# Upper slots of V filled earlier, whole-chunk remainders on VectorE, and one plain fp32 chunk in eight

## The chip, the cores and the metric

The kernel runs on one core of one Trainium2 chip. The metric is the device time of one execution in microseconds; of several runs the median is taken.

## The reference, cut to what matters

One inference step of a one-layer decoder: 264 live tokens (256 prompt tokens, 8 samples) and 16 meta tokens, everything in fp32. After attention, convolution and an output projection comes the PEER mixer, which is the part that the change touches:

```python
def peer_ffn(h, w_query, sub_keys, expert_u, expert_v):
    ...
        top_s, pos = lax.top_k(cand_s, PEER_TOPK)
        idx = jnp.take_along_axis(cand_i, pos, axis=-1)
        gate = jax.nn.softmax(top_s, axis=-1).astype(hc.dtype)
        act = jax.nn.gelu(jnp.einsum('cd,chkd->chk', hc, expert_u[idx]))
        return jnp.einsum('chk,chkd->cd', gate * act, expert_v[idx])
    ...
```

There are 16384 experts; each token takes 16 of them for each of 8 heads, so 128. `expert_u` and `expert_v` have one row of 2048 numbers for each expert.

## The kernel before, in words

**Stages.** The input projection, attention, the output projection and the query projection come first. Then stage U multiplies all of `expert_u` with the tokens, in 64 pairs of tiles (`PAIR_QRY` to `PAIR_U`), and stage V multiplies all of `expert_v` with weights W, from 1550.61 us to 2170.58 us. U and the projections cut their matrices into an fp32r rounded part (`hi`, made by ScalarE) and a remainder (`lo`, made by VectorE: raw minus `hi`), and run three products per tile.

**Stage V.** The tokens are in two kinds. For TD = 184 of them W is dense: 128 rows by 184 columns for each of 128 chunks of experts. For the other TG = 80 only the 128 chosen rows of `expert_v` are fetched by indirect DMA on GpSimd's queue (`gather_rows`, tile `gat`, a ring of ROWS = 4 buffers) and VectorE adds each into `gacc`, times the weight `gw` (`add_rows`, an "addition" below). These weights need words that GpSimd gathers too (`gather_u`, tile `gu`): 80 of them, one or two behind each of the first rows. GpSimd's order is fixed, and a row's gather waits until the addition four before it is done. V runs in two passes over the halves of the 2048 output columns, each with 128 chunks in 16 turns of 8 and 80 additions. All of `expert_v` passes through 8 slots of 512 KB: four in `raw`, which U uses too, and four upper ones in `raw_v`.

**A chunk on TensorE.** A split chunk is two quarters (`f`, L2225 and L2230): four matmuls of `hi` against the rounded and the remaining part of W side by side (368 columns), then four of `lo` against the rounded part of W (184 columns). A chunk whose number mod 8 is in `NATIVE` is plain (`plain`, L2240): eight products in plain fp32, each in two instructions, and neither ScalarE nor VectorE touches it. In both passes that is number 3 and number 7 of a turn; one of these is split all the same, the very last.

**What ScalarE and VectorE do beside it.** Their programs are written out in `halves`: at step k of a turn come the two quarters that lie 3 and 4 ahead (so the second quarter of the next chunk, and the first of the one after it), at each even k the parts of W for the chunk pair from k+2 on (`w_part`, tile `whl`), and then what `between` holds for this step: at k = 3 of pass 0's first four turns a product with counts (`times_up`), and at the steps listed in the table `ADDS` an addition. `hi` and `lo` have four buffers of a quarter each, so a quarter's parts may be written when TensorE is done with the quarter four before it. At the start of pass 1 the sums of pass 0 are added (L2119, turn 0), and in its turn 13 stand two reductions (L2129). Near the end of each pass TensorE multiplies `gacc` into the result (`row_sums`, L2212), between the products of the last quarters; it waits once for the last addition before that (`SUMS_AT`).

**What sets the order.** Each engine has one queue in program order. SP issues all loads; `load_expert` waits until a slot's former chunk is split (or, for a plain chunk, multiplied). `BOUNDS` and `WORDS_AT` say at the start of which turns the weights of which additions are made.

## Time and profile before

| | |
|---|---|
| median of 3 runs | 2191.46 us (2189.42 to 2191.72) |
| the profiled execution | 2187.61 us, its span 2185.9 us |
| TensorE busy | 2155.6 us, 99% |
| VectorE busy | 1618.8 us, 74% |
| ScalarE busy | 1120.7 us, 51% |
| GpSimd busy | 786.1 us, 36% |
| plain products of V (L2240) | 1008 instructions, 63 chunks |
| additions (L2094) | 160, 1278 ns each |
| remainders in V (L1627) | 383 records, 685 to 690 ns each |
| mean granted clock of TensorE | 0.991 of full |

The times of the profiled execution are read against its own 2187.61 us. Busy shares are means over stages with different limits: what stage V is worth is read from the timelines within it. A line such as L2225 is a line of the kernel before.

### The profile page before, as it was taken

To read this page: it belongs to the slowest core of one execution; us is meant where nothing else is said; L and a number is where in the kernel's file an instruction comes from. 1 tells how busy PE (TensorE), PEld (TensorE's weight loads), DVE (VectorE), ACT (ScalarE), POOL (GpSimd) and SP (SyncE) were. 2 spreads that over 40 slices of the span, in tenths; PEclk is the share of its full clock that TensorE was granted. 3 is DMA by queue.
4 is the path that set the end of the run, shared out by engine and by line. 5 is a ranking of instruction groups with operands and counts; after the bars stand their busy time and mean duration, and the time that the engine had idled before them with its cause. 6 is when DMAs were issued, how large, how long until landed. Compare 5 with 4: busy or idle time off the path is not lost.

```text
span 2185.9 us, 53083 instructions
## 1 busy us (share of the span) xinstructions
PE 2155.6 (99%) x16578; PEld 2123.5 (97%) x16578; DVE 1618.8 (74%) x2988; ACT 1120.7 (51%) x2094; POOL 786.1 (36%) x612
## 2 busy tenths in 40 slices
PE   9999999999999999999999999999999999999997
PEld 8999899999999999999999999999999999999997
DVE  8788788886766767888886444466588888888885
ACT  6445366667555444555555444444444444444453
POOL 0321100002011000588888888500377743222230
PEclk9999999999999999999999999999999999999997
DMA  7887756666555655777777877789899999999993
GB/s 247 290 290 250 238 179 196 190 214 216 186 187 191 192 167 180 190 190 181 190 191 188 191 187 186 186 272 287 275 378 378 372 390 400 327 370 369 367 370 142
DMA packets 302250, 546.01 MB, mean 250 GB/s; under 512 B 76896, under 2 KB 114232, under 8 KB 302016
## 3 DMA queue, kind: packets, MB, share of 16 engines
q1 hardware_dynamic: 225440, 427.67, 59.8%
q0 software_dynamic: 60064, 105.07, 16.1%
q10 hardware_dynamic: 16640, 12.06, 1.8%
q8 instruction: 41, 0.67, 0.1%
q14 instruction: 65, 0.53, 0.1%
HBM read 519.39 MB, written 25.28 MB: 249 GB/s over the span
## 4 chain that ended last, share of the span: by engine, by line
PE 66%; POOL 5%; issue 2%; DMA 2%; DVE 1%; ACT 0%; DVEq 0%; SPq 0%; ACTq 0%
PE ps L319 16%; PE ps L322 15%; PE ps L318 15%; PE ps L2225 8%; PE ps L2240 5%; PE ps L2230 5%; POOL gu L1801 3%; POOL gat L1643 2%; DMA gat<-expert_v,gidx 1%; DMA raw_v<-expert_v 0%; DMA raw<-weights 0%; PE ps L2212 0%; PE ps L1405 0%; DVE gacc L2094 0%; DVE lo L1627 0%
## 5 line engine op out<-in xcount | busy, mean ns | idle before, releaser
L306 DVE TENSOR_TENSOR lo<-raw,hi 128x512 fp32r<-128x512 f32 x995 | 685.6, 696 | 367.4 <-ACT hi L301 345.0
L301 ACT CAST hi<-raw 128x512 fp32r<-128x512 f32 x995 | 608.0, 619 | 472.7 <-PE ps L322 447.5
L318 PE MATMUL ps<-h_hi,hi 128*128 128x264 f32 (+1 forms) x3200 | 821.4, 286 | 1.6 <-DVE h_lo L959 1.6
L319 PE MATMUL ps<-h_lo,hi 128*128 128x264 f32 (+1 forms) x3200 | 820.2, 286 | 0.0
L318 PEld LDWEIGHTS ps<-h_hi,hi 128*128 128x128 f32 x3200 | 601.8, 188 | 9.0 <-issue 6.0
L319 PEld LDWEIGHTS ps<-h_lo,hi 128*128 128x128 f32 x3200 | 601.9, 188 | 0.0
L1784 POOL DMA_INDIRECT w_spill<-chosen,widx x256 | 432.4, 1689 | 264.8 <-DVE widx L2007 187.1
L322 PE MATMUL ps<-h_hi,lo 128*128 128x264 f32 (+1 forms) x3200 | 523.3, 285 | 2.0 <-DVE lo L306 1.8
L322 PEld LDWEIGHTS ps<-h_hi,lo 128*128 128x128 f32 x3200 | 444.3, 188 | 3.7 <-DVE lo L306 3.4
L2225 PE MATMUL ps<-whl,hi 128*128 128x368 f32 x1544 | 346.3, 345 | 4.6 <-DVE gacc L2094 2.8
L1643 POOL DMA_INDIRECT gat<-expert_v,gidx x160 | 179.6, 1123 | 285.2 <-DVE gacc L2094 269.6
L2225 PEld LDWEIGHTS ps<-whl,hi 128*128 128x128 f32 x1544 | 252.3, 192 | 6.0 <-DVE gacc L2094 3.1
L2230 PE MATMUL ps<-whl,lo 128*128 128x184 f32 x1544 | 227.9, 270 | 1.8 <-DVE lo L1627 1.6
L2230 PEld LDWEIGHTS ps<-whl,lo 128*128 128x128 f32 x1544 | 224.8, 191 | 3.3 <-DVE lo L1627 3.3
L2094 DVE SCALAR_TENSOR_TENSOR gacc<-gat,gw,gacc 128x1024 f32<-128x1024 f32 x160 | 204.5, 1278 | 9.0 <-DMA gat<-expert_v,gidx 9.0
L1622 ACT CAST hi<-raw_v 128x512 fp32r<-128x512 f32 x194 | 120.2, 620 | 163.7 <-PE ps L2230 120.4
L1622 ACT CAST hi<-raw 128x512 fp32r<-128x512 f32 x189 | 117.1, 620 | 160.3 <-PE ps L2230 109.7
L1627 DVE TENSOR_TENSOR lo<-raw,hi 128x512 fp32r<-128x512 f32 x189 | 127.1, 690 | 58.7 <-ACT hi L1622 50.7
L1627 DVE TENSOR_TENSOR lo<-raw_v,hi 128x512 fp32r<-128x512 f32 x194 | 128.0, 685 | 47.8 <-ACT hi L1622 47.7
L1801 POOL DMA_INDIRECT gu<-u_spill,gidx x80 | 91.1, 1139 | 177.1 <-issue 177.1
L1067 DVE SCALAR_TENSOR_TENSOR yc<-cv,dw,yc 128x256 f32<-128x256 f32 x240 | 107.1, 477 | 0.1
L1824 ACT ACTIVATE W<-ps 128x184 f32 (+1 forms) x128 | 41.4, 324 | 106.2 <-PE ps L322 105.8
(308 smaller groups left out, 2301.6 us busy)
## 6 DMA issues: line engine op xcount, KB each, us to landing
raw<-u_tiles SPq DMA_DIRECT2D x512, 256.0 KB
raw<-weights SPq DMA_DIRECT2D x480, 256.0 KB
raw_v<-expert_v SPq DMA_DIRECT2D x128, 512.0 KB
raw<-expert_v SPq DMA_DIRECT2D x124, 512.0 KB
w_spill<-zeros ACTq DMA_DIRECT2D x16, 736.0 KB, 5.7
wld<-w_spill SPq DMA_DIRECT2D x32, 368.0 KB, 4.1
u_spill<-ust SPq DMA_DIRECT2D x128, 40.0 KB
qb<-q_spill POOLq DMA_DIRECT2D x8, 512.0 KB, 6.0
```

Source lines behind the costliest of these rows:

```text
L301: nc.scalar.copy(hi[k % SPLIT][:], raw_quarter(k)).then_inc(hi_done, 1)
L306: nc.vector.tensor_tensor(lo[k % SPLIT][:], raw_quarter(k), hi[k % SPLIT][:].bitcast(F32), ALU.subtract).then_inc(lo_done, 1)
L318: pe.matmul(out, a, rhs[0][:, first + j, 0:n], start=start and j == 0, stop=False)
L319: pe.matmul(out, a, rhs[1][:, first + j, 0:n], start=False, stop=False)
L322: m = pe.matmul(out, lo[k % SPLIT][:, j], rhs[0][:, first + j, 0:n], start=False, stop=stop and j == QT - 1)
L1622: nc.scalar.copy(hi[q % SPLIT][:], expert_quarter(q)).then_inc(hi_done, credit(q))
L1627: nc.vector.tensor_tensor(lo[q % SPLIT][:], expert_quarter(q), hi[q % SPLIT][:].bitcast(F32), ALU.subtract).then_inc(lo_done, credit(q))
L1643: nc.gpsimd.indirect_dma_start(gat[n % ROWS][:], None, v_rows, bass.IndirectOffsetOnAxis(ap=index, axis=0)).then_inc(gat_in[n % ROWS], 16)
L1784: nc.gpsimd.indirect_dma_start(w_cells, bass.IndirectOffsetOnAxis(ap=widx[0:n, t, hd, k:k + 1], axis=0), chosen[0:n, 2, t, hd, k:k + 1], N ...
L2094: nc.vector.scalar_tensor_tensor(out=gacc[:, g], in0=gat[b][:], scalar=gw[:, j:j + 1], in1=gacc[:, g], op0=ALU.mult, op1=ALU.add).then_inc ...
L2225: pe.matmul(ps[:, bank(QT * r + j), 0:2 * TD], a[:, j], whl[k // 2 % 2][:, k % 2].rearrange("p a n -> p (a n)"), start=start, stop=False, ...
L2230: m = pe.matmul(ps[:, bank(QT * r + j), 0:TD], b[:, j], whl[k // 2 % 2][:, k % 2, 0], start=False, stop=stop, skip_group_check=True)
```

## The change

Three things are changed. The first loads of the upper slots (chunks 4 to 7 of V) are issued in the last four pairs of U instead of at V's start; they count on semaphores of their own (`piece_in`, which the input's pieces used before). In V the remainder of a chunk is one subtraction over both its quarters, at the place where its second quarter's stood; only the first quarters of V stay as they were. And `NATIVE` is `(7,)`: chunk 3 of every turn is split. Beside these the additions are spread in another way (`ADDS`), and so are the turns in which their weights are made.

```diff
-NATIVE = (3, 7)
+NATIVE = (7,)
...
-    BOUNDS = (1, 2, 4, 7, 10, 13)
+    BOUNDS = (1, 2, 4, 6, 8, 11)
     FIVE, SIX = (1, 2, 3, 5, 6), (1, 2, 3, 5, 6, 7)
-    ADDS = [[(), (3, 5, 6, 7)] + 6 * [FIVE] + 6 * [SIX] + [FIVE, (0, 1, 2, 3, 4)], 15 * [FIVE] + [(0, 1, 2, 3, 4)]]
-    WORDS_AT = (0, 5, 15, 30, 50, 65, TG)
+    AT_END = (0, 1, 2, 3, 4)
+    ADDS = [[(), (2, 3, 5, 6, 7)] + [SIX if i in (4, 7, 9, 11, 13) else FIVE for i in range(2, 15)] + [AT_END],
+            [SIX if i in (3, 8, 12) else FIVE for i in range(15)] + [AT_END[0:2]]]
+    WORDS_AT = (0, 5, 15, 30, 40, 55, TG)
...
     def expert_lo(dve, q):
+        if q % 2 == 0:
+            return
         dve.wait_ge(hi_done, 2 * C0 + q + 2 * RAW + 1)
         dve.wait_ge(mm_done, 2 * C0 + q + 1)
-        nc.vector.tensor_tensor(lo[q % SPLIT][:], expert_quarter(q), hi[q % SPLIT][:].bitcast(F32),
-                                ALU.subtract).then_inc(lo_done, credit(q))
+        if q < AHEAD + 1:
+            nc.vector.tensor_tensor(lo[q % SPLIT][:], expert_quarter(q), hi[q % SPLIT][:].bitcast(F32),
+                                    ALU.subtract).then_inc(lo_done, credit(q))
+            return
+        both = slice((q - 1) % SPLIT, q % SPLIT + 1)
+        rows = expert_slot(q // 2 % SLOTS).rearrange("p (r j) n -> p r j n", r=2)
+        nc.vector.tensor_tensor(lo_parts[:, both], rows, hi_parts[:, both].bitcast(F32),
+                                ALU.subtract).then_inc(lo_done, 1 + credit(q))
...
+        def upper_in(s):
+            sp.dma_start(expert_slot(s).rearrange("p a b -> p (a b)"), expert_v[0, s]).then_inc(expert_in(s), 16)
+
+        def weighed_pair(i, upper=None):
             for s in range(RAW):
                 load_half(sp, 4 * i + s, s, u_tiles[4 * (i - PAIR_QRY) + s])
...
+                if s == 0 and upper:
+                    upper_in(upper)
+        with sp.Fori(PAIR_W, PAIR_U - 4) as i:
+            weighed_pair(i)
+        for i in range(PAIR_U - 4, PAIR_U - 1):
+            weighed_pair(i, RAW + i - PAIR_U + 4)
```

On SP's queue at the end of U and the start of V stood, before, these rows (`raw<-expert_v` of 128x512 are half-chunk loads of chunks 0 to 3, `raw_v<-expert_v` loads of the upper slots, `ust` and `wld` U's results and counts):

```order
L1669 DMA u_spill<-ust_76 128x80
L291 DMA raw<-expert_v 128x512 x4
L1669 DMA u_spill<-ust_77 128x80
L291 DMA raw<-expert_v 128x512 x4
L1669 DMA u_spill<-ust_76 128x80
L1672 DMA wld<-w_spill 128x4x184
L1739 DMA raw_v<-expert_v 128x1024
L1669 DMA u_spill<-ust_77 128x80
L1739 DMA raw_v<-expert_v 128x1024 x2
L1739 DMA raw<-expert_v 128x1024 x3
L1739 DMA raw_v<-expert_v 128x1024
L1672 DMA wld<-w_spill 128x4x184
```

Now the last pair of U has this, with the last of the four upper loads behind the first half-loads of the pair:

```order
L1687 DMA wld<-w_spill 128x4x184
L292 DMA raw<-u_tiles 128x512 x2
L1719 DMA raw_v<-expert_v 128x1024
L292 DMA raw<-u_tiles 128x512 x2
L1684 DMA u_spill<-ust_71 128x80
L1687 DMA wld<-w_spill 128x4x184
L292 DMA raw<-u_tiles 128x512 x4
L1684 DMA u_spill<-ust_70 128x80
L292 DMA raw<-expert_v 128x512 x4
L1684 DMA u_spill<-ust_71 128x80
L292 DMA raw<-expert_v 128x512 x4
L1684 DMA u_spill<-ust_70 128x80
```

and right behind it follow:

```order
L1687 DMA wld<-w_spill 128x4x184
L1764 DMA raw<-expert_v 128x1024
L1684 DMA u_spill<-ust_71 128x80
L1764 DMA raw<-expert_v 128x1024 x2
L1687 DMA wld<-w_spill 128x4x184
L1764 DMA raw<-expert_v 128x1024
```

So no load of chunks 4 to 7 stands behind U's last results any more, and SP goes on with chunks 8 to 15.

On VectorE, the first part of a turn of pass 1 with five additions (all such turns read alike; `whl` of 128x2x184 are the parts of W for two chunks, of 128x184 for one):

```order
L1627 TENSOR_TENSOR lo_57<-raw,hi_53 128x512
L1627 TENSOR_TENSOR lo_54<-raw,hi_50 128x512
L2086 TENSOR_TENSOR whl_160<-W,whl_160 128x184
L1627 TENSOR_TENSOR lo_55<-raw,hi_51 128x512
L2094 SCALAR_TENSOR_TENSOR gacc<-gat_151,gw,gacc 128x1024
L1627 TENSOR_TENSOR lo_54<-raw_v,hi_50 128x512
L2086 TENSOR_TENSOR whl_159<-W,whl_159 128x2x184
L2094 SCALAR_TENSOR_TENSOR gacc<-gat_164,gw,gacc 128x1024
L1627 TENSOR_TENSOR lo_55<-raw_v,hi_51 128x512
L1627 TENSOR_TENSOR lo_56<-raw_v,hi_52 128x512
L2094 SCALAR_TENSOR_TENSOR gacc<-gat_165,gw,gacc 128x1024
L1627 TENSOR_TENSOR lo_57<-raw_v,hi_53 128x512
```

and the same part now, from the end of the turn before it:

```order
L1642 TENSOR_TENSOR lo<-raw,hi 128x1024 x2
L2108 TENSOR_TENSOR whl_154<-W,whl_154 128x2x184
L1642 TENSOR_TENSOR lo<-raw,hi 128x1024
L2116 SCALAR_TENSOR_TENSOR gacc<-gat_147,gw,gacc 128x1024
L1642 TENSOR_TENSOR lo<-raw,hi 128x1024
L2108 TENSOR_TENSOR whl_153<-W,whl_153 128x2x184
L2116 SCALAR_TENSOR_TENSOR gacc<-gat_145,gw,gacc 128x1024
L1642 TENSOR_TENSOR lo<-raw_v,hi 128x1024
L2116 SCALAR_TENSOR_TENSOR gacc<-gat_158,gw,gacc 128x1024
L1642 TENSOR_TENSOR lo<-raw_v,hi 128x1024
L2108 TENSOR_TENSOR whl_154<-W,whl_154 128x184
```

Between two additions there stands now one subtraction over 1024 elements where two over 512 stood, and chunk 3, which was passed over, has its subtraction and its part of W too.

## Rows read from the trace of the kernel before

**Rows 1.** Busy time by stage: span, each engine's busy us, clock, DMA share, GB/s.

```profile
1444.10:1455.80 11.70, 11.70 (x99) 11.70 (x98) 9.39 (x14) 6.51 (x14) 0.00 (x0) 1.00 1.04 355
1502.60:1514.30 11.70, 11.70 (x98) 11.70 (x97) 7.98 (x11) 5.76 (x13) 0.00 (x0) 1.00 0.91 281
1900.00:1950.00 50.00, 50.00 (x350) 50.00 (x349) 40.99 (x57) 22.73 (x43) 14.18 (x14) 1.00 1.02 366
```

**Rows 2.** Timeline of TensorE in pass 1: start, length, line, operation, count.

```profile
1904.70 2.68 PE L2240 MATMUL ps<-W,raw 128*128 x16
...
1907.09 0.97 PE L2225 MATMUL ps<-whl,hi 128*128 128x368 f32 x4
...
1909.45 0.86 PE L2225 MATMUL ps<-whl,hi 128*128 128x368 f32 x4
1910.15 0.59 PE L2230 MATMUL ps<-whl,lo 128*128 128x184 f32 x4
...
1913.93 2.68 PE L2240 MATMUL ps<-W,raw_v 128*128 x16
```

**Rows 3.** Timeline of TensorE in V's first turn.

```profile
1570.61 4.12 PE L2240 MATMUL ps<-W,raw_v 128*128 128x184 f32 x16 [3.82 <-DMA raw_v<-expert_v]
```

**Rows 4.** Timeline of GpSimd while it gathers rows and words.

```profile
1576.15 0.99 POOL L1801 DMA_INDIRECT gu<-u_spill,gidx  x1 [0.30 <-issue]
...
1586.71 1.15 POOL L1643 DMA_INDIRECT gat<-expert_v,gidx  x1 [9.57 <-DVE gacc L2094]
...
1745.57 0.94 POOL L1643 DMA_INDIRECT gat<-expert_v,gidx  x1 [0.30 <-issue]
```

**Rows 5.** Timeline of VectorE: row additions 0, 45 and 47 of pass 0.

```profile
1585.17 1.28 DVE L2094 SCALAR_TENSOR_TENSOR gacc<-gat,gw,gacc 128x1024 f32<-128x1024 f32 x1
...
1745.65 1.28 DVE L2094 SCALAR_TENSOR_TENSOR gacc<-gat,gw,gacc 128x1024 f32<-128x1024 f32 x1 [1.26 <-DMA gat<-expert_v,gidx]
...
1752.43 1.28 DVE L2094 SCALAR_TENSOR_TENSOR gacc<-gat,gw,gacc 128x1024 f32<-128x1024 f32 x1 [0.39 <-DMA gat<-expert_v,gidx]
```

**Rows 6.** Timeline of TensorE: first and last chunk of turn 10.

```profile
1743.42 0.97 PE L2225 MATMUL ps<-whl,hi 128*128 128x368 f32 x4
...
1761.46 0.81 PE L2240 MATMUL ps<-W,raw_v 128*128 x4
```

**Rows 7.** Timeline of VectorE in pass 1, a turn with five additions.

```profile
1904.48 0.69 DVE L1627 TENSOR_TENSOR lo<-raw_v,hi 128x512 fp32r<-128x512 f32 x1 [1.38 <-ACT hi L1622]
...
1905.09 0.53 DVE L2086 TENSOR_TENSOR whl<-W,whl 128x368 fp32r<-128x368 f32 x1
...
1905.54 1.28 DVE L2094 SCALAR_TENSOR_TENSOR gacc<-gat,gw,gacc 128x1024 f32<-128x1024 f32 x1
...
1906.74 1.28 DVE L1627 TENSOR_TENSOR lo<-raw_v,hi 128x512 fp32r<-128x512 f32 x2
...
1910.34 0.34 DVE L2086 TENSOR_TENSOR whl<-W,whl 128x184 fp32r<-128x184 f32 x1
```

**Rows 8.** Timeline of ScalarE in the same turn.

```profile
1904.35 0.50 ACT L1834 CAST whl<-W 128x368 fp32r<-128x368 f32 x1
...
1909.72 0.62 ACT L1622 CAST hi<-raw_v 128x512 fp32r<-128x512 f32 x1 [0.28 <-PE ps L2230]
```

**Rows 9.** Timeline of VectorE in turn 13 of pass 1.

```profile
2113.91 2.21 DVE L2129 TENSOR_REDUCE total<-half_sum 128x132 f32<-128x1056 f32 x1
```

**Rows 10.** Timeline of TensorE: row sums of pass 0, then of pass 1.

```profile
1851.89 0.60 PE L2225 MATMUL ps<-whl,hi 128*128 128x368 f32 x2 [0.24 <-DVE gacc L2094]
...
1853.97 0.53 PE L2225 MATMUL ps<-whl,hi 128*128 128x368 f32 x2
...
2152.37 0.98 PE L2225 MATMUL ps<-whl,hi 128*128 128x368 f32 x2 [2.52 <-DVE gacc L2094]
...
2156.27 0.87 PE L2225 MATMUL ps<-whl,hi 128*128 128x368 f32 x2
```

**Rows 11.** Busy time by stage, row sums of pass 1.

```profile
2156.20:2160.00 3.80, 3.80 (x18) 3.80 (x18) 0.69 (x1) 0.62 (x1) 0.00 (x0) 0.50 0.02 4
```

More of the change, by code:

```diff
@@ L1731, in load_expert @@
             m = NK * p + 8 * i + s
-            first = isinstance(i, int) and p == 0 and i == 0
-            back = m - (RAW if first else SLOTS)
+            back = m - SLOTS
             if native(back if isinstance(i, int) else s + SLOTS):
```

35 lines of the change are left out of this document (18 added, 17 removed).

## Prediction

> **What bounds the kernel now.** I read the busy time by stage first. In U's last pairs and in V TensorE is busy all the time at full clock [rows 1]; so it sets the end, except where it stands still. VectorE is busy 41 of 50 us in V, the nearest of the others. Then I read TensorE's timeline in V for what one chunk costs and for each place where it stops, and then, at these places, the engine that it waits for.
>
> A half turn is 9.23 us: three split chunks of 2.24 us (two from 1909.45 to 1913.93), and the rest, 2.51 us, is the plain chunk, which ends at 1907.09 and makes the group behind it 0.11 longer [rows 2]. A turn is 18.46 us.
>
> TensorE stops for long at three places. In V's first turn chunk 7 is not there: 3.82 us of idle time, and its products then take 4.12 us instead of 2.68 [rows 2, 3]: 5.3 us. Around turn 10 it waits for VectorE, and VectorE for gathered rows [rows 5]. Before the last row sums it waits 2.52 us for the last addition, and the quarters behind that take 3.90 us where the same in pass 0 take 2.08 [rows 10], at a granted clock of 0.50, so 1.2 GHz [rows 11].
>
> **What the change does, part by part.**
>
> *Early upper slots.* They take the first stop away. What they add to U is one load of 512 KB in each of four pairs of 11.70 us, 45 GB/s on top of 281, where the same mix ran at 355 GB/s without TensorE waiting [rows 1]. I take 0 for U. That V's first turn is 5.3 us shorter is true, but a later part gives it no use:
>
> *The pace of the gathers.* GpSimd issues a row every (1745.57 - 1586.71) / 43 = 3.69 us, since one or two words stand between rows, and in this whole stretch it waits for nobody (0.30 us between its instructions) [rows 4]. It starts at 1586.71 because it waited 9.57 us for addition 0, which ran at 1585.17 [rows 4, 5]. Now addition 0 stands one step earlier in a turn that begins 5.3 us earlier with one more cheap chunk, so at about 1576; then GpSimd's own last word (1576.15 + 0.99 + 0.30) sets the start, 1577.4, 9.3 us earlier. But the new table wants more from it: in turns 1 to 9 stand 48 additions instead of 46. At 3.69 us each, the last of turn 9 is now number 47, issued at 1577.4 + 158.9 = 1736.3. Before, number 47 ran 6.86 us after its issue, having waited for the landing [rows 4, 5]: that gives 1743.2, and I take 1 us more, since its landing was a quick one. Turn 10 can begin 0.5 us ahead of that addition: behind it stand 1.20 (its time to the next instruction, 1906.74 - 1905.54 [rows 7]), the subtraction for the turn's second chunk, 1.27, and 0.1 for loading, against 2.35 + 0.70 us after which TensorE wants it [rows 2]. So turn 10 begins at about 1743.7; before it began at 1743.42 [rows 6]. **Up to turn 10: +0.3 us** (bounds -1 and +2). The 5.3 us, and all that turns 1 to 9 might gain, are gone, spread over many short waits for rows.
>
> Turn 10 took 1761.46 + 2.39 - 1743.42 = 20.43 us [rows 2, 6], 2 us of it stalls, since VectorE was behind. The gathers of words are over by now in the new order, so it is a usual turn: **-1.9 us**.
>
> *A usual turn after the change.* For TensorE it is 7 x 2.24 + 2.51 = 18.19, 0.27 less. Whether it gets that depends on VectorE. A subtraction over 512 holds VectorE 0.61, an addition 1.20, parts of W 0.45 for two chunks, 0.26 for one [rows 7]. A subtraction over 1024 isn't in the trace. Above it is bounded by two of 512, 1.22. The step between 128x184 and 128x368 is 0.19 for 184 elements, so 0.53 for 512; twice that with no fixed part at all is 1.06, the bound below. I take 0.61 + 0.53 = 1.14, and its result is there 0.08 later, as with the others. The Trainium skill, VectorE: DVE Perf Modes, section on the TRN2 errata, gives (N + 151) / 0.96 ns for the whole length of such an fp32 operation, 1.22 us; by it nothing in the sum would be different.
>
> So VectorE does 7 x 1.14 + 3 x 0.45 + 0.26 + 5 x 1.20 = 15.6 us in 18.2: it fits. But in steps 1 to 3 it has 3 x (1.14 + 1.20) + 0.45 = 7.5 us to do in 6.7, and its head start is small, as the remainder of a chunk's first quarter now comes only with the second: that can't begin before TensorE has left the chunk two back, plus 0.27 and 0.62 for ScalarE's `hi` [rows 8]. With the turn's start as 0, TensorE begins its chunks at 0, 2.35, 4.59, 6.83, 9.07 and so on. Step 1: subtraction 3.30 to 4.44, addition to 5.64. Step 2: to 6.78; then it waits for ScalarE's part of W, which follows a `hi` that waits for the first quarter of chunk 2 (5.71 + 0.27 + 0.52 + 0.50 = 7.00) [rows 8]; to 7.50, addition to 8.70. Step 3: subtraction from 8.70, to be read at 9.97. TensorE wants it at 9.07 + 0.70 = 9.77, better 0.1 before. **It stalls for about 0.35 us once in a turn**; in step 4 there is no addition and VectorE catches up. The turn is 18.54, against 18.46: +0.08. A sixth addition at step 7 falls into slack. Bounds: 18.19 (no stall) and 18.8 (two more near misses of 0.1).
>
> Turns 11 to 15 of pass 0 and 16 of pass 1 remain. 17 of them are usual: **+1.4 us**. The rest by the same walk: pass 0's last turn, with additions at steps 0 to 4, stalls 1.0: +0.5. Pass 1's first, with four sums of 0.6 us between: stalls 1.3: +1.1. Its turn 13, with two reductions of 2.1 us [rows 9], in which VectorE starts late by 0.9, 0.1, 0.6, 0.1 and 1.3 us: 2.9 of stalls, +2.3. The last, almost without additions: -0.3. **Together +3.6 us.**
>
> *The end.* Only two additions stand in the last turn, at steps 0 and 1, so the wait of 2.52 us before the row sums is gone. Without that gap the clock shouldn't fall: in pass 0 the same products, entered after 0.24 us of idle time, run in 2.08 us a quarter [rows 10]. Four quarters give 4 x 1.82 = 7.3: **-9.8 us**.
>
> **The sum:** +0.3 - 1.9 + 1.4 + 3.6 - 9.8 = -6.4 us, from 2187.61 to 2181.2 for an execution like the profiled one. That one stands 3.85 us below the median; from the median it is 2185.0.
>
> **The rivals.**
>
> *VectorE keeps up* (20%): the walk is too strict by some tenths, which is all that it needs. Then 18 turns gain 0.35 each and the special ones half of theirs: -8, so 2177. For it: VectorE is idle 18% of the time. Against it: the same walk through the old turn puts its second addition 7.7 us behind the turn's start (1904.70 - 6.84), and there the trace has it, at 1905.54 [rows 2, 7].
>
> *The gathers don't hold V back* (10%): landings come sooner or GpSimd issues faster. Then most of the 5.3 us and of nine turns' 0.2 are kept: 2179. Against it: GpSimd had no gap to give [rows 4].
>
> *The clock falls at the end all the same* (10%): +7.3, so 2192. The Trainium skill, TensorE: Matmul & The Clock Gate, Part 1, says that the clock falls behind idle time and comes back with sustained work; by this it would stay up here, and the trace agrees: 0.50 behind the gap of 2.52 us [rows 11].
>
> *The late remainder costs more* (15%), the one on the slower side: as TensorE waits for both quarters' remainder before the first quarter's second group, any delay of `hi`, of a row's landing or of an addition is handed on undamped, where the old order had over 1 us to spare. If a usual turn is 19.1 instead of 18.54 and the special ones double: +10 + 3, so 2198. From 19.0 on it decides: the change is then slower.
>
> **How the numbers follow.** My own case has 45% and its range is 2180 to 2190. No change that a measurement of this kernel can tell is within 0.2%, 2187.1 to 2195.8. Below that lie six tenths of my case and the first two rivals, 0.57, less a little for both: 0.55. Above lie the last rival and a part of the clock's: 0.17. The range 2174 to 2197 leaves out the ends of the first and the last rival.
>
> **What would show it.** In the profile after: no wait of TensorE for `raw_v`; GpSimd's fifth row at about 1577 and its 48th at about 1736, and TensorE waiting for `lo` in turns 2 to 9, with turn 10 beginning near 1743.7; from there turns of 18.5 us with one wait for `lo` each, in the fifth chunk; a pass 1 turn 13 of 21 us; no wait before the last row sums, and quarters of 2.1 us there. It would be wrong if the turns were 18.2 or 19 us, if turn 10 began before 1740, or if the clock at the end were 0.50.

## The result, and the profile after the change

The changed kernel took 2200.1 us (median; 2194.8 to 2210.7, apart from one run of 9209), the kernel before, beside it, 2189.9 us. The ratio is 1.0052, with a 95% interval of 1.0042 to 1.0062: **slower**, by 0.5%, 10.2 us between the two medians. The forecast was 2185.0 us, with a range up to 2197: wrong in its sign, and outside its range. The profiled execution took 2199.36 us with a span of 2197.6; before it was 2187.61 and 2185.9, so the two traces differ by 11.8 us, 1.6 more than the medians, and can be laid side by side.

I read in the order in which the forecast went. First TensorE's timeline in V's first turns (start, length, line, operation, count, and in brackets the idle time ahead and who ended it), the rows that answer to [rows 3]:

```profile
1581.35 0.69 PE L2252 MATMUL ps<-whl,lo 128*128 128x184 f32 x4 [0.67 <-DVE lo L1642]
1596.96 1.16 PE L2252 MATMUL ps<-whl,lo 128*128 128x184 f32 x4 [6.07 <-DVE lo L1642]
```

No wait for `raw_v` is left: the first turn's chunk 7 is there when it is wanted. But in turn 2 stands a stop of 6.07 us, longer than the one removed. It is for a remainder, and VectorE, which makes it, shows why it is late:

```profile
1587.12 1.22 DVE L1642 TENSOR_TENSOR lo<-raw,hi 128x1024 fp32r<-128x1024 f32 x1
1593.76 1.28 DVE L2116 SCALAR_TENSOR_TENSOR gacc<-gat,gw,gacc 128x1024 f32<-128x1024 f32 x1 [5.42 <-DMA gat<-expert_v,gidx]
1595.68 1.23 DVE L1642 TENSOR_TENSOR lo<-raw,hi 128x1024 fp32r<-128x1024 f32 x1
```

The fifth addition waited 5.42 us for its row (row 4, counted from 0), and the subtraction queued behind it came with it. Behind this stop the granted clock is down as well, 0.57 on the mean from 1597 to 1603 us (length, each engine's busy us, clock, DMA share, GB/s):

```profile
1597.00:1603.00 6.00, 6.00 (x26) 6.00 (x27) 3.91 (x4) 1.88 (x4) 4.78 (x5) 0.57 0.93 256
```

A group of products with the rounded part takes 1.49 us there, elsewhere 0.86. So the next view is GpSimd's timeline, the rows that answer to [rows 4]:

```profile
1576.08 1.72 POOL L1823 DMA_INDIRECT gu<-u_spill,gidx  x1 [0.30 <-issue]
1578.11 1.66 POOL L1658 DMA_INDIRECT gat<-expert_v,gidx  x1 [0.31 <-issue]
1580.08 3.43 POOL L1823 DMA_INDIRECT gu<-u_spill,gidx  x1 [0.30 <-issue]
1583.81 0.94 POOL L1823 DMA_INDIRECT gu<-u_spill,gidx  x1 [0.30 <-issue]
1585.06 0.95 POOL L1658 DMA_INDIRECT gat<-expert_v,gidx  x1 [0.30 <-issue]
...
1748.85 1.96 POOL L1658 DMA_INDIRECT gat<-expert_v,gidx  x1 [0.30 <-DVE gacc L2116]
```

GpSimd waits for nobody (0.30 us between instructions), yet row 4 is issued at 1585.06, where 1577.4 was forecast, and row 47 at 1748.85 instead of 1736.3. Its instructions have become long: 1.72, 1.66, one of 3.43. The groups of instructions say it for the whole kernel, before (first fence) and after: 1123 and 1534 ns for the same gather (count, then busy us and mean ns of one). Most of this rise stands where the rows aren't awaited: over rows 4 to 47 alone the mean is 1.19 us before and 1.26 after, over pass 1 it is 1.11 and 1.67.

```profile
L1643 POOL DMA_INDIRECT gat<-expert_v,gidx x160 | 179.6, 1123 | 285.2 <-DVE gacc L2094 269.6 <-issue 15.5
```

```profile
L1658 POOL DMA_INDIRECT gat<-expert_v,gidx x160 | 245.5, 1534 | 224.4 <-DVE gacc L2116 208.8 <-issue 15.5
L1642 DVE TENSOR_TENSOR lo<-raw,hi 128x1024 fp32r<-128x1024 f32 x126 | 153.8, 1222 | 15.8 <-ACT hi L1629 14.8 <-PE ps L2252 0.6
L1642 DVE TENSOR_TENSOR lo<-raw_v,hi 128x1024 fp32r<-128x1024 f32 x97 | 118.5, 1221 | 6.3 <-ACT hi L1629 4.6
```

Second, TensorE around turn 10 and in a usual turn of pass 1, the rows that answer to [rows 6] and [rows 2]. The 16 products of a plain chunk end a turn:

```profile
1753.94 2.68 PE L2262 MATMUL ps<-W,raw_v 128*128 x16
1756.33 0.97 PE L2247 MATMUL ps<-whl,hi 128*128 128x368 f32 x4
...
1909.59 2.68 PE L2262 MATMUL ps<-W,raw_v 128*128 x16
1911.98 0.97 PE L2247 MATMUL ps<-whl,hi 128*128 128x368 f32 x4
...
1921.11 0.86 PE L2247 MATMUL ps<-whl,hi 128*128 128x368 f32 x4
1922.04 0.69 PE L2252 MATMUL ps<-whl,lo 128*128 128x184 f32 x4
...
1928.26 2.06 PE L2262 MATMUL ps<-W,raw_v 128*128 x12
```

Turn 10 begins at 1756.33, against 1743.42 before [rows 6]. The usual turn is 1928.26 - 1909.59 = 18.67 us, against 18.46. Its products need 18.19; the rest are small waits, of which the largest is at 1922.04, in the fifth chunk: products of the remainder that begin 0.93 us behind the group ahead of them, where the others begin 0.70 behind. With the slower group behind it, this one costs 0.33 us.

Third, the end, the rows that answer to [rows 10]:

```profile
2172.40 0.56 PE L2234 MATMUL ps<-same,gacc 128*128 128x16 f32 x4
...
2174.41 0.56 PE L2234 MATMUL ps<-same,gacc 128*128 128x16 f32 x4
...
2176.42 0.55 PE L2234 MATMUL ps<-same,gacc 128*128 128x16 f32 x4
```

A quarter takes 2.01 us where it took 3.90, nothing waits ahead of them, and the granted clock between 2172 and 2182 is 1.00.

So the change's own gain at the end is there, and what is lost lies in turns 1 to 9, and in small pieces behind.

### The profile page after: what moved, and what is told of

Same layout as the page of the kernel before. It is cut to its first block and busy times, and to the rows that moved or that the text cites. A ratio compares the mean times of both kernels' runs of the same rounds, so it can differ in the third digit from the quotient of the medians.

```text
span 2197.6 us, 52837 instructions
## 1 busy us (share of the span) xinstructions
PE 2154.8 (98%) x16578; PEld 2102.6 (96%) x16578; DVE 1650.6 (75%) x2829; ACT 1165.3 (53%) x2158; POOL 859.3 (39%) x612
## 5 line engine op out<-in xcount | busy, mean ns | idle before, releaser
L307 DVE TENSOR_TENSOR lo<-raw,hi 128x512 fp32r<-128x512 f32 x995 | 686.0, 697 | 366.2 <-ACT hi L302 342.9
L302 ACT CAST hi<-raw 128x512 fp32r<-128x512 f32 x995 | 608.0, 619 | 471.8 <-PE ps L323 445.2
L2247 PE MATMUL ps<-whl,hi 128*128 128x368 f32 x1800 | 393.8, 340 | 0.8 <-DVE whl L2108 0.5
L1658 POOL DMA_INDIRECT gat<-expert_v,gidx x160 | 245.5, 1534 | 224.4 <-DVE gacc L2116 208.8
L2252 PEld LDWEIGHTS ps<-whl,lo 128*128 128x128 f32 x1800 | 255.3, 191 | 45.5 <-DVE lo L1642 38.9
L2252 PE MATMUL ps<-whl,lo 128*128 128x184 f32 x1800 | 274.3, 274 | 22.5 <-DVE lo L1642 20.4
L2247 PEld LDWEIGHTS ps<-whl,hi 128*128 128x128 f32 x1800 | 289.8, 191 | 1.1 <-DVE whl L2108 0.7
L1629 ACT CAST hi<-raw 128x512 fp32r<-128x512 f32 x253 | 156.8, 620 | 205.5 <-PE ps L2252 160.9
L1642 DVE TENSOR_TENSOR lo<-raw,hi 128x1024 fp32r<-128x1024 f32 x126 | 153.8, 1222 | 15.8 <-ACT hi L1629 14.8
L1642 DVE TENSOR_TENSOR lo<-raw_v,hi 128x1024 fp32r<-128x1024 f32 x97 | 118.5, 1221 | 6.3 <-ACT hi L1629 4.6
L2108 DVE TENSOR_TENSOR whl<-W,whl 128x368 fp32r<-128x368 f32 (+1 forms) x128 | 63.1, 493 | 60.5 <-PE ps L2252 49.1
```

Source lines behind the costliest of these rows:

```text
L302: nc.scalar.copy(hi[k % SPLIT][:], raw_quarter(k)).then_inc(hi_done, 1)
L307: nc.vector.tensor_tensor(lo[k % SPLIT][:], raw_quarter(k), hi[k % SPLIT][:].bitcast(F32), ALU.subtract).then_inc(lo_done, 1)
L1629: nc.scalar.copy(hi[q % SPLIT][:], expert_quarter(q)).then_inc(hi_done, credit(q))
L1642: nc.vector.tensor_tensor(lo_parts[:, both], rows, hi_parts[:, both].bitcast(F32), ALU.subtract).then_inc(lo_done, 1 + credit(q))
L1658: nc.gpsimd.indirect_dma_start(gat[n % ROWS][:], None, v_rows, bass.IndirectOffsetOnAxis(ap=index, axis=0)).then_inc(gat_in[n % ROWS], 16)
L2247: pe.matmul(ps[:, bank(QT * r + j), 0:2 * TD], a[:, j], whl[k // 2 % 2][:, k % 2].rearrange("p a n -> p (a n)"), start=start, stop=False, ...
```

## The experiments

Two suspects, both of one edit, the single subtraction for a whole chunk. **Theory 1**: VectorE's longer instruction holds off GpSimd, so that rows come late while they set the pace. **Theory 3**: TensorE gets the first quarter's remainder half a microsecond later, and stalls in each turn. Against both, **theory 2**: GpSimd is late because the change asks more of it and of VectorE. The runs went in four sets, each beside runs of the kernel before on its own chip. The chips differ: the kernel before took 2188.8 us in the first set, 2197.4, 2197.8 and 2195.9 in the others (the last two sets are one chip). So ratios are compared, and places in the traces. A ratio is of medians; a place in a trace (the last four columns) is of one execution.

| run | set | ratio to before (95%) | row 4 issued | turn 9's plain chunk | usual turn, pass 1 | gather, mean ns |
|---|---|---|---|---|---|---|
| before | | 1 | 1586.71 | 1741.03 | 18.45 | 1123 |
| the change | | 1.0052 (1.0042-1.0062) | 1585.06 | 1753.94 | 18.67 | 1534 |
| two subtractions | 1 | 0.9963 (0.9949-0.9978) | 1577.29 | 1742.76 | 18.19 | 1406 |
| single subtraction alone | 1 | 1.0061 (1.0042-1.0080) | 1584.64 | 1745.74 | 18.67 | 1362 |
| back to back | 1 | 0.9973 (0.9959-0.9987) | 1578.28 | 1747.53 | 18.19 | 1302 |
| early slots + additions | 1 | 0.9958 (0.9945-0.9971) | 1578.48 | 1744.89 | 18.45 | 1170 |
| late release | 2 | 0.9993 (0.9981-1.0006) | 1576.78 | 1746.24 | 18.88 | 1209 |
| single from turn 10 | 2 | 0.9986 (0.9972-0.9999) | 1577.90 | 1743.21 | 18.67 | 1446 |
| later demand | 2 | 0.9963 (0.9947-0.9980) | 1578.26 | 1737.77 | 18.19 | 1339 |
| the change again | 3 | 1.0019 (1.0003-1.0035) | 1583.21 | 1752.48 | 18.67 | 1492 |
| rounded parts first | 3 | 1.0015 (0.9997-1.0033) | 1577.26 | 1750.95 | 18.66 | 1623 |
| plain 3, later demand | 3 | 0.9956 (0.9939-0.9973) | 1576.66 | 1737.22 | 18.45 | 1132 |
| additions alone | 3 | 0.9978 (0.9963-0.9994) | 1583.56 | 1752.59 | 18.45 | 1131 |
| single up to turn 9 | 4 | 1.0018 (1.0001-1.0035) | 1583.66 | 1754.69 | 18.19 | 1339 |
| early slots alone | 4 | 0.9979 (0.9963-0.9995) | 1578.89 | 1737.89 | 18.45 | 1123 |
| two subtractions again | 4 | 0.9964 (0.9947-0.9980) | 1577.78 | 1746.33 | 18.19 | 1355 |
| early slots + additions again | 4 | 0.9948 (0.9929-0.9967) | 1574.63 | 1741.71 | 18.45 | 1162 |

**Two subtractions.** The change without the single subtraction:

```diff
-        if q % 2 == 0:
-            return
...
-        nc.vector.tensor_tensor(lo_parts[:, both], rows, hi_parts[:, both].bitcast(F32),
-                                ALU.subtract).then_inc(lo_done, 1 + credit(q))
+        nc.vector.tensor_tensor(lo[q % SPLIT][:], expert_quarter(q), hi[q % SPLIT][:].bitcast(F32),
+                                ALU.subtract).then_inc(lo_done, credit(q))
```

> The change whole, but the rounded parts are again subtracted a quarter at a time (128x512), as before the change. Theory 1 (the one 128x1024 subtraction of 1.22 us holds off GpSimd's gather instructions, so that rows are issued and land later in the turns in which the rows set the pace): a gather's instruction falls back from 1534 ns to about 1.14 us in pass 0 and 1.1 us in pass 1, row 47 of pass 0 is issued by about 1737 instead of 1748.85, turn 10 begins by about 1744 instead of 1756.3, the usual turn of pass 1 is 18.1 to 18.4 us instead of 18.67, and the end keeps its clock: 2177 to 2181 us. Theory 2 (GpSimd is slow because the change asks it for rows sooner, and VectorE has one more split chunk a turn to serve): the gather's instruction stays above 1.3 us and turn 10 begins at 1752 or later: 2190 to 2198 us.

2177.95 us, 0.9963: the single subtraction turns a gain of 0.37% into a loss of 0.52%. Row 4 is issued at 1577.29, as forecast for the change:

```profile
1577.29 1.15 POOL L1649 DMA_INDIRECT gat<-expert_v,gidx  x1 [0.58 <-DVE gacc L2107]
1578.74 1.14 POOL L1814 DMA_INDIRECT gu<-u_spill,gidx  x1 [0.30 <-issue]
1580.18 2.96 POOL L1814 DMA_INDIRECT gu<-u_spill,gidx  x1 [0.30 <-issue]
```

But theory 1 had more to say and missed: the gather's mean is 1406 ns, not 1.1 us, and row 47 comes at 1741.04, not 1737. The gather's mean over the kernel is no measure of the loss: here it is 1.58 us in pass 1, where GpSimd waits for VectorE anyhow, and 1.10 us over rows 4 to 47. Nor is the one of 3.43 us the change's own: one of 2.96 stands here too, but behind row 4. The 11.2 us by which turn 9's plain chunk comes sooner than in the change (1742.76 against 1753.94) are 7.8 at row 4, nothing in the 43 rows behind it (163.75 and 163.79 us), and 3.4 between row 47 and that chunk.

**The single subtraction alone**, on the kernel before (the same lines the other way round, and the buffers of `hi` and `lo` side by side).

> The kernel before, with the one 128x1024 subtraction for a chunk as the only change: chunks 3 and 7 stay plain, the table of additions and the late upper slots stay as they were. Theory 1: a gather's instruction rises from 1123 ns to 1.35 us or more, more so in pass 1, and turn 10 begins 6 us or more later than 1743.42: 2194 to 2202 us in all. Theory 2: the gather's instruction stays within 0.05 us of 1123 ns, VectorE has 0.12 us a chunk less to do, and the time is that of before within 3 us.

2198.81 us, 1.0061. Theory 1's time, with turn 9's plain chunk 4.7 us later than before (6 or more were expected) and the usual turn 18.67 instead of 18.45, although two plain chunks a turn leave VectorE more time. Theory 2, by which this kernel would be as fast as before, has fallen.

**Early slots and additions**, with chunk 3 left in plain fp32 (`NATIVE = (3, 7)`) and two subtractions.

> The kernel before with the early upper slots and the new table of additions; the subtraction stays a quarter at a time and chunk 3 stays in plain fp32. Theory 1: gathers at about 1.14 us, no stop for raw_v in the first turn, turn 10 begins by 1744, the end keeps its clock (about 9.8 us gained there): 2178 to 2183 us. Theory 2: the new table asks for rows sooner than GpSimd has them, gathers above 1.3 us, turn 10 at 1750 or later: 2186 to 2194 us.

2178.68 us, 0.9958: gathers short (1170 ns), no stop for `raw_v`, the end at full clock. Turn 9's plain chunk is at 1744.89, later than I expected, since rows are still short in number: VectorE waited 4.26 us for row 23. But whether TensorE's turn is 18.45 or 18.19 us, the two kernels without the single subtraction are within 0.1% of each other in this set.

**Two subtractions, back to back.** The waits of the change, its instruction cut in two:

```diff
+        for r in range(2):
+            one = slice((q - 1) % SPLIT + r, (q - 1) % SPLIT + r + 1)
+            nc.vector.tensor_tensor(lo_parts[:, one], rows[:, r:r + 1], hi_parts[:, one].bitcast(F32),
+                                    ALU.subtract).then_inc(lo_done, credit(q) if r else 1)
```

> The change whole, but the subtraction of a chunk is given as two instructions of 128x512, one straight after the other once the whole chunk is rounded: the waits and their order are those of the change, only the length of one instruction is halved (0.67 us each). If the length of the single instruction holds GpSimd off (theory 1 in its narrow form), a gather's instruction falls to 1.2 us or less and the time to 2178 to 2186 us. If what holds it off is the unbroken stretch in which VectorE subtracts, however many instructions it is made of (theory 1 in its wide form), the gather's instruction stays at 1.4 us or more and the time at 2197 to 2203. If the loss is that the first quarter's remainder comes late to TensorE (theory 3), it is 2198 to 2204 too, with gathers that have become short.

2181.57 us, 0.9973: nearly all is back, though VectorE does more (its gathers, at 1302 ns, are longer than the 1.2 us that I had named). It isn't the wait for the whole chunk's rounding that costs, but that one instruction does both quarters.

**Late release.** The same two instructions, but neither quarter is released until both are done (`then_inc(lo_done, 1 + credit(q))` on the second alone).

> As the run with two subtractions back to back (2181.6 us), but the first quarter's remainder is released only with the second's, as in the change; each instruction stays 128x512. In the last runs a usual turn of pass 1 was 18.19 us with that quarter released after the first of the two, and 18.67 in the change. Theory 3 (the late remainder holds TensorE): the usual turn is 18.7 to 18.8 us, 0.08 us of VectorE more than the change per chunk, and the whole 2195 to 2202 us. Theory 1 (only GpSimd's delay by the long instruction counts): the usual turn stays at 18.19 and the whole near 2182.

The usual turn goes from 18.19 to 18.88 us: theory 3, by itself. The rows are on time (row 4 at 1576.78, gathers of 1209 ns). The time, 0.9993, lies between. In VectorE's timeline of this run the subtraction that TensorE waits for stands behind a part of W and an addition, with no idle time between them:

```profile
1970.69 0.54 DVE L2112 TENSOR_TENSOR whl<-W,whl 128x368 fp32r<-128x368 f32 x1 [0.47 <-issue]
1971.15 1.28 DVE L2120 SCALAR_TENSOR_TENSOR gacc<-gat,gw,gacc 128x1024 f32<-128x1024 f32 x1
1972.35 1.29 DVE L1644 TENSOR_TENSOR lo<-raw_v,hi 128x512 fp32r<-128x512 f32 x2
```

```profile
1972.34 0.86 PE L2251 MATMUL ps<-whl,hi 128*128 128x368 f32 x4
1973.69 0.69 PE L2256 MATMUL ps<-whl,lo 128*128 128x184 f32 x4 [0.49 <-DVE lo L1644]
```

The first of the two takes 0.69 us from 1972.35 and would have served TensorE at 1973.04; it was told at the end of both. In the change, with one instruction of 1.22 us instead of 1.29, it is the same with a little less.

**The single subtraction only from turn 10 on**, and its complement, **only up to turn 9** (`q >= 16 * 10`, and `q < 16 * 10`, as the condition for it).

> The change, with the single subtraction of a chunk only from pass 0's turn 10 on; up to there a quarter at a time. If the loss has two parts, turns 1 to 9 (rows late) and 0.48 us in each turn after, then turns 1 to 9 go as in the run with two subtractions (turn 10 begins by about 1746 instead of 1756.3), the usual turn of pass 1 is 18.67, its turns 13 and 14 take 42.7 together, and the whole is 2186 to 2190 us. If the single subtraction costs only where rows set the pace: 2177 to 2181. If it costs only behind turn 10: 2197 to 2200.

> The change with the single subtraction of a chunk only in turns 0 to 9 of pass 0, a quarter at a time from turn 10 on: the complement of the run with it from turn 10 on only. If the two costs add up: turn 10 begins at 1752 to 1757 as in the change (1756.3 and 1754.9 in its two profiles) against 1745 to 1747 without it, row 4 is issued at 1583 to 1585, the usual turn of pass 1 is 18.19 us, its turn 13 20.7; the span is 8 to 10 us above that of the run with two subtractions, 12 to 13 below the change's. If the rows' lateness has nothing to do with the single subtraction, turn 10 begins by 1747 and the span is that of two subtractions.

The traces part cleanly. Up to turn 9's plain chunk the first stands where two subtractions stand (1743.21 and 1742.76), the second where the change does (1754.69 and 1753.94, against 1746.33 for two subtractions in its own set: 8.4 us). From there to the plain chunk of turn 14 of pass 1 the first takes 2148.90 - 1743.21 = 405.7 us, two subtractions 2136.49 - 1742.76 = 393.7; the second takes 396.6, and two subtractions in its set 398.1. The change's trace against that of two subtractions in the first set is 11.2 us later up to there and loses 10.2 more behind: in the traces there are two costs, of like size. The medians don't part them as cleanly. They give 0.54% (1.0018 against 0.9964) up to turn 9, and about 0.22% (0.9986 against 0.9964, from two chips) behind. But on the last chip the change itself has 1.0019, no more than the run up to turn 9: there the medians show nothing of the second cost. And the traces of these two runs are of quick executions: up to turn 9, 2192.88 us, the fastest of its twelve and 5.7 below their median; from turn 10 on, 2190.42 us, 4.2 below. Of the totals, the first was forecast 5 us too low (2186 to 2190, measured 2194.6); the second's span, 2191.1, is 7.2 us above two subtractions, near the 8 to 10 expected, but only 4.8 below the change again, not 12 to 13: on that chip two subtractions lose something behind turn 10 that the change doesn't, of which more below.

**Gathers beside VectorE**, the disputed cost by itself.

> A kernel of its own, which computes nothing of the reference (its outputs are zeros): seven stretches, in each of which GpSimd issues eight indirect gathers of 128 rows of 1024 while VectorE (1) rests, (2) subtracts 128x512 from SBUF 24 times without a pause, (3) subtracts 128x1024 12 times without a pause, (4) 128x512 with a pause after each, (5) 128x1024 with a pause after each, (6) subtracts 128x512 with one input from PSUM, without a pause, (7) makes the addition's operation 128x1024 without a pause. Theory 1: 0.94 us a gather at rest; beside a VectorE that never pauses each gather is held to the end of the run or for several us (2, 3, 7 alike); with pauses 1.1 to 1.3 us beside 128x512 and 1.4 to 1.7 beside 128x1024; and 0.94 in (6) if it is the second SBUF input that holds it. Theory 2 (GpSimd isn't touched by VectorE): 0.94 in all.

GpSimd's timeline, with one gather of each of the stretches 1 (at rest), 3 (128x1024, no pause), 4 (128x512, pauses) and 5 (128x1024, pauses):

```profile
10.82 0.94 POOL L56 DMA_INDIRECT gat<-v,idx  x1 [0.31 <-issue]
...
56.62 1.96 POOL L62 DMA_INDIRECT gat<-v,idx  x1 [0.30 <-issue]
...
78.78 1.32 POOL L65 DMA_INDIRECT gat<-v,idx  x1 [0.30 <-issue]
...
94.14 1.18 POOL L68 DMA_INDIRECT gat<-v,idx  x1 [0.30 <-issue]
```

At rest a gather takes 0.94 us; beside subtractions of 128x1024 without a pause 1.97, and 1.97 + 0.30 is two of VectorE's steps (12 of them span 13.7 us, 1.14 each): every gather ends 0.94 us into a subtraction, as if it had stood still until that one began. Theory 1 has its mechanism. But two of my numbers missed. A VectorE that never pauses doesn't lock GpSimd out, and beside 128x512 without a pause, or the additions without a pause, one gather in eight was held (1.38 us) and the others took 0.94: two steps of 128x512 (24 took 14.8 us, 0.62 each) or one addition (12 took 14.7, 1.23) are nearly GpSimd's own step at rest, 1.24, so that it falls in step. What a hold costs hangs on how two rhythms meet. That also left one thing unproved: all gathers beside the input from PSUM took 0.93 or 0.94, but at the same rhythm as those that were hardly held anyway. So a second kernel put both inputs side by side.

> As the run of gathers beside VectorE, computing nothing of the reference (outputs are zeros). Eight gathers in each of seven stretches, beside a VectorE that (1) rests, (2) subtracts 128x1024 without a pause, second input from PSUM, (3) the same, both inputs from SBUF, (4) and (5) the same two with a pause after each, (6) and (7) 128x512 from PSUM and from SBUF with a pause after each. If the second SBUF input holds GpSimd off: 0.94 us a gather in 1, 2, 4 and 6; 1.97 in 3; about 1.18 in 5; 0.94 and 1.32 in turn in 7. If the rhythm or the output's writing does it, whatever the input: 2 as 3, 4 as 5, 6 as 7.

The groups of its gathers, in the order of the stretches 2 to 7 (each is line, count, busy us, mean ns of one):

```profile
L59 POOL DMA_INDIRECT gat<-v,idx x8 | 7.5, 937 | 20.9 <-DMA gat<-v,idx 18.8 <-issue 2.1
L62 POOL DMA_INDIRECT gat<-v,idx x8 | 13.0, 1626 | 9.5 <-DMA gat<-v,idx 7.4 <-issue 2.1
L65 POOL DMA_INDIRECT gat<-v,idx x8 | 7.5, 936 | 8.1 <-DMA gat<-v,idx 5.9 <-issue 2.1
L68 POOL DMA_INDIRECT gat<-v,idx x8 | 9.6, 1200 | 10.1 <-DMA gat<-v,idx 8.0 <-issue 2.1
L71 POOL DMA_INDIRECT gat<-v,idx x8 | 7.5, 936 | 8.4 <-DMA gat<-v,idx 6.3 <-issue 2.1
L74 POOL DMA_INDIRECT gat<-v,idx x8 | 9.2, 1144 | 9.8 <-DMA gat<-v,idx 7.6 <-issue 2.1
```

Input from PSUM 937, 936, 936 ns; from SBUF, at the same width and rhythm, 1626, 1200 and 1144. It is the second input in SBUF that holds GpSimd off, in these runs until the instruction underway is over. In the kernel a gather can be held longer: the one of 3.43 us began at 1580.08, beside a subtraction, outlasted that one, a part of W and a second subtraction, and ended 0.91 us into the addition behind them. Why it wasn't let in sooner isn't shown. The Trainium skill (SBUF — State Buffer, section "Who interferes with whom") says that a VectorE instruction with two SBUF inputs contends with a GpSimd instruction that reads SBUF, and these runs agree. The same section infers that such a subtraction doesn't stall a DMA that GpSimd issues; here the measurement decides otherwise.

**Rounded parts first.** The change, with TensorE's order in a split chunk turned round, so that it wants the first remainder later:

```diff
+        def both_first(c, k):
+            pe.wait_ge(wlo_done, c + 1)
+            for r in range(2):
+                pe.wait_ge(hi_done, 2 * C0 + 2 * c + r + 2 * RAW + 1)
...
+            pe.wait_ge(lo_done, 2 * C0 + 2 * c + 1 + 2 * RAW + 1)
+            for r in range(2):
```

> The change, with TensorE's order inside a split chunk turned round in turns 1 to 14 of both passes: first the products of the rounded part for both quarters, then those of the remainder for both; so TensorE wants the first remainder 0.75 us later. VectorE's single subtraction is as in the change. Theory 3 (0.48 us a turn comes from TensorE having to wait for a remainder that the single subtraction brings late): the usual turn of pass 1 falls from 18.67 to 18.19 us, and what stays of the loss is turns 1 to 9 with rows that come late (gathers still long, 1.5 to 1.7 us in pass 1): 0.999 to 1.002 of before. If the 0.48 us come from something else in VectorE (its total load), the turn stays at 18.67 and the ratio at 1.005.

A miss: the usual turn stayed at 18.66, the ratio at 1.0015 (the change in its set: 1.0019). VectorE's timeline tells what happened. In this run's usual turn, which begins at 1913.44, its second part of W is at

```profile
1916.78 0.54 DVE L2108 TENSOR_TENSOR whl<-W,whl 128x368 fp32r<-128x368 f32 x1 [0.80 <-ACT whl L1856]
```

which is 3.34 us after the turn's start; in the change it was

```profile
1914.65 0.54 DVE L2108 TENSOR_TENSOR whl<-W,whl 128x368 fp32r<-128x368 f32 x1 [0.35 <-PE ps L2252]
```

2.67 us after it. TensorE wants the remainder 0.75 later, but it also lets go of the first quarter's buffers that much later, so ScalarE's `hi`, its part of W, and VectorE behind them all begin later. What the one end gained the other lost. That TensorE's wait for a remainder told late is what lengthens the turn is so shown only by the late release, beside the run back to back: the same instructions, and 18.88 us against 18.19.

**Later demand**: two subtractions, five additions in each of turns 1 to 9 and six in each of turns 10 to 14 (`8 * [FIVE] + 5 * [SIX]`), and the same with chunk 3 in plain fp32.

> The change without the single subtraction, and with the sixth additions moved behind turn 9: five additions in each of turns 1 to 9 (45 instead of 48) and six in each of turns 10 to 14 of pass 0. In the run with two subtractions turns 0 to 9 took 16 us more than ten of 18.19, with rows at 3.8 us each. If the rows' demand sets these stops, three rows fewer are worth 3 x 3.8 = 11 us less what the six additions a turn cost VectorE behind: turn 10 begins about 1737 to 1740, and the whole is 2168 to 2174 us. If the stops come from VectorE's own load or from single late rows, turn 10 begins as before (1745) and the whole is 2176 to 2180.

> The early upper slots and the new table of additions without the single subtraction and with chunk 3 in plain fp32, and the table as in the run with later demand: five additions in each of turns 1 to 9, six in each of turns 10 to 14. There turn 10 began 5 us earlier, but each of turns 10 to 14 took 19.3 us instead of 18.19, since VectorE had six additions beside fourteen subtractions. With twelve subtractions a turn it should keep up: turn 10 begins at about 1740, turns 10 to 14 take 18.46 to 18.7, and the whole is 0.993 to 0.995 of before (with the table of the change: 0.9958). If VectorE still falls behind: 0.996.

The rows' part came out: turn 9's plain chunk at 1737.77 and 1737.22, 5.0 and 7.7 us sooner than with the change's table (1742.76, 1744.89). Both gave it back: turns 10 to 14 took 18.5 to 20.3 us in the first, turns 11 to 14 19.5 to 20.5 in the second. In the second the last turn of pass 0 and the first of pass 1 took 24.9 us each as well, where the kernel before has 20.7 and 21.0. I had put that down to VectorE and its six additions, and expected the second to be free of it (0.993 to 0.995) and the first to take 2168 to 2174 us, 0.991 to 0.993 of before. The waits from 1757 to 1856 us, of the first and of the second, say otherwise:

```profile
ACT hi L1628 <- DMA raw<-expert_v: 28.6, 17, 3.7
ACT hi L1628 <- DMA raw_v<-expert_v: 15.0, 15, 1.4
```

```profile
ACT hi L1628 <- DMA raw_v<-expert_v: 25.5, 14, 3.8
ACT hi L1628 <- DMA raw<-expert_v: 21.6, 12, 3.7
```

ScalarE waits for the expert chunks themselves. A turn loads eight of 512 KB, and with six rows of the same size it asks more of the DMA engines than with five. Measured are 0.9963 and 0.9956, and neither beats the change's own table.

**The change again, the additions alone, the early slots alone**, and the two best once more.

> The change itself once more, on the chip of the runs beside it, since the chips differ: before had a median of 2188.8 us in one set of runs and 2197.4 in another. Expected 1.003 to 1.007 of before, and the same places of loss: row 4 issued about 8 us later than in the run with two subtractions back to back and late release (1576.8), usual turns of pass 1 at 18.67 us.

> The kernel before with the new table of additions alone (the upper slots filled late, as before; two subtractions a chunk; chunk 3 plain). The end should keep its clock and lose its wait (9.8 us gained), the stop for raw_v in the first turn stays, row 4 is issued no earlier than 1577, and the two additions more in turns 1 to 9 cost up to 7 us of stops: 0.997 to 1.000 of before, against 0.9958 with the early upper slots as well. If the early slots are given no use, it is 0.996.

> The kernel before with the early upper slots alone: the table of additions is that of before, chunk 3 plain, two subtractions. The prediction says that the 3.8 us stop for raw_v goes, but that the rows, which GpSimd issues at its own pace from addition 0 on, give it back by turn 10. Addition 0 then still stands at step 3 of turn 1, so row 4 is issued at about 1581 to 1582 (1586.71 less the 5.3 us), and turn 10 begins 5 us earlier, at 1738 to 1739, if GpSimd is carried forward with it: 0.9975 of before. If it is given back: turn 10 at 1743 and 0.999 to 1.001. The end stays at 1.2 GHz with its wait of 2.5 us.

> The change with two subtractions a chunk, once more on this chip: 0.9963 of before if the gain is the kernel's and not the chip's. If expert loads land late on this chip (ScalarE waiting for raw and raw_v, as in the last runs with later demand), a turn of 18.19 us asks for more than one of 18.67 and part of the gain is lost: 0.997 to 0.999.

> The early upper slots and the new table of additions alone, once more on this chip: 0.9958 of before, equal to the run with two subtractions within 0.1%, since there the 0.27 us a turn of chunk 3 went into waits for rows and for VectorE. Its turns are 18.46 us.

The change keeps its absolute time, 2200.3 us, while the kernel before is 9 us slower here than in the first set; hence 1.0019, below what I expected. What differs, two subtractions on this chip show: they keep turns of 18.19 us up to turn 7 of pass 1, and then take 18.2 to 20.4 where the first set had 18.19. The waits between 2010 and 2120 us, of this run and then of the change again:

```profile
ACT hi L1628 <- DMA raw<-expert_v: 27.4, 19, 4.2
ACT hi L1628 <- DMA raw_v<-expert_v: 14.2, 14, 1.6
```

```profile
ACT hi L1629 <- PE ps L2252: 40.4, 52, 2.8
DVE whl L2108 <- PE ps L2252: 10.1, 10, 1.4
```

The first waits for expert loads, the second for TensorE. Busy time from 2010 to 2120 us, of two subtractions in the first set and here (length, each engine's busy us, clock, DMA share, GB/s):

```profile
2010.00:2120.00 110.00, 108.75 (x760) 107.48 (x759) 102.84 (x142) 64.58 (x123) 46.85 (x32) 1.00 1.01 384
```

```profile
2010.00:2120.00 110.00, 106.75 (x728) 103.64 (x727) 96.91 (x133) 58.68 (x114) 35.93 (x30) 1.00 1.01 372
```

The DMA engines are busy all the time in both, and bring 384 GB/s on one chip and 372 on the other, where the loads come late. The share alone doesn't tell this: it is 1.00 as well in the change again, which moves 363 GB/s on that chip and doesn't wait for loads. So a turn of 18.19 us asks for more than one of 18.67, and I take it that this chip hadn't more to give; that the chip is the cause, and not the execution, is argued and not shown. Whether the kernel before loses its 9 us there in the same way wasn't traced. The ratio didn't suffer: 0.9964, where I had expected 0.997 to 0.999 if the loads came late.

The additions alone (0.9978) and the early slots alone (0.9979) multiply to 0.9957; together they measured 0.9958 and 0.9948 (the second 0.16% below two subtractions in its set, where 0.1% at most was expected). In the additions alone turn 9's plain chunk begins at 1752.59, 11.6 us later than before and nearly as late as in the change, though their gathers are short (1131 ns): their row 4, behind the stop for `raw_v`, is issued at 1583.56, and the new table wants two rows more. So a late row 4 is enough for this loss, whatever makes it late, and beside the new table the early slots do have a use: they bring row 4 to 1578.48 and 1574.63, and the chunk to 1744.89 and 1741.71. With the early slots alone row 4 was issued at 1578.89, sooner than I had it (1581 to 1582), and turn 9's plain chunk is 3.1 us sooner than before, where 5 were expected if GpSimd is carried along and none if not: the truth is between. The best of all kernels is thus **the early slots and the new table, without the single subtraction and with chunk 3 left in plain fp32**: 2178.68 us in the first set, 0.42% (0.52% in the last) below the kernel before. Splitting chunk 3 as well makes TensorE's turn 0.26 us shorter and brings nothing (0.9963, 0.9964).

## Why the prediction was wrong, point by point

In pieces of the profiled execution, the change against before, with the forecast in brackets: up to turn 10 +12.9 us (+0.3); turn 10 itself -1.3 (-1.9); sixteen usual turns +3.8 (+0.08 each, +1.4 for seventeen); pass 0's last +0.4 (+0.5), pass 1's first +0.8 (+1.1); its turn 13 +3.1 (+2.3), turn 14 +2.4 (a usual one); the rest to the end -10.4 (-9.8 and -0.3). The sum is +11.7, against 11.75 measured (2199.36 - 2187.61).

- **The step that failed is the pace of the gathers**, +0.3 us, in which GpSimd's instructions keep their length whatever VectorE does. Of its error of 12.6 us, 7.7 are the restart: row 4 at 1585.06 instead of 1577.4. In the kernel with two subtractions it is at 1577.29, so that number was right for a VectorE whose subtractions stay short. With the single one, 1585.06 and 1583.21 in two traces of the change and 1583.66 in the run up to turn 9. The other 4.9 are the pace: 163.8 us for 43 rows instead of 158.9. That isn't the single subtraction's: it is 162.8 to 164.8 us with two subtractions and with early slots and additions, 163.56 with the early slots alone, and 163.1 with the additions alone. What makes it longer than the 158.86 of before isn't shown. The step from row 47 to turn 10, 7.4 us, measured 7.48, and that is luck: it is 4.1 us with two subtractions and 8.3 with the additions alone, so of the 11.2 us between the change and two subtractions 3.4 arise there.
- **The early slots** take the stop away, as said. "Given no use" was too strict: alone they make the kernel 0.21% faster (0.9979, down to 0.9963 and up to 0.9995), and turn 9's plain chunk begins 3.1 us sooner, of 5.3.
- **The usual turn** was right in its mechanism and its place, the fifth chunk, for want of the first quarter's remainder, and even in the size of that stall: 0.33 us for 0.35. But there are two smaller ones, of 0.07 and 0.10, that only the upper bound had in it, and a sixth addition doesn't fall into slack: the turn behind one is up to 0.1 us longer. So turns take 18.65 to 18.78 us, not 18.54. From turn 10 to turn 13 of pass 1, special turns with it, this is 3.5 us more than forecast.
- **Turn 14 of pass 1** has a single late row: VectorE waited 2.06 us for a landing. The change again has 18.67 there, and the run from turn 10 on 18.68; nothing was foretold of such, and I leave it as chance.
- **The end** was right: -10.4 for -10.1, the clock at 1.00.
- **The rivals.** "The late remainder costs more" was the one on the right side, with 15%. It decided from a turn of 19.0, and the turn was 18.67: the late remainder makes most of the loss behind turn 10 and could not alone have done it. GpSimd held off, which makes the loss up to turn 10, was in no rival. Rival "the gathers don't hold V back" had the sign wrong.

What could have been seen in the trace before: the gathers weren't all of one length. At rest 0.94, they had a mean of 1123 ns, and of the three in [rows 4] one took 1.15. I took the pace as GpSimd's own and didn't ask who made it.

What stays open: how the loss parts in the medians, as said; why the two rhythms meet so badly just between 1562 and 1585 us (rounded parts first, with the same long subtraction, issued row 4 at 1577.26, and lost its time at a later pace of 171.6 us for 43 rows); no run here controls it. And whether GpSimd would be spared if the rounded part stood in PSUM: not tried.

## What to carry to other kernels

Joining two instructions saves little, here 0.10 us in a step of 1.24, and costs twice: the consumer of the first half gets it half an instruction later, and GpSimd's gathers are held for the longer length, if both inputs of the joined instruction lie in SBUF. Do it only where neither is on the path. A gain that ends in a stage paced by another engine is to be costed with that engine's instruction lengths beside the new instructions, not with its old mean. And when a kernel's DMA share is already 1.0, a shorter turn must be timed on more than one chip.

## What the runs showed of the hardware that I had not expected

- An indirect gather on GpSimd takes 0.94 us at rest, up to 1.97 beside fp32 subtractions of 128x1024 with both inputs in SBUF, 1.45 at most beside 128x512 with pauses, and 0.93 to 0.94 when one input is in PSUM. Among the kernel's mixed instructions single gathers took 2.96 and 3.43.
- Beside an unbroken row of 128x512 subtractions seven of eight stay at 0.94: the cost comes from where the rhythms meet, not from VectorE's load.
- The same subtraction costs 0.69 us over 512 and 1.22 to 1.23 over 1024, with steps of 0.62 and 1.14: joining two saves 0.1 us.
- At a DMA share of 1.0 the same kernel had its expert loads late in the trace from one chip and not in the one from another: turns of up to 20.4 us instead of 18.19. The share was 1.0 at 363 GB/s without such waits, and at 372 with them.
